# Prompt queries formed by pairs of heads, their rotated part for all heads at once and brought to the heads' rows by DMA

## The reference, cut to what matters

```python
q = (rmsnorm(c_q, ln_q) @ w_q_b).reshape(b, t, N_HEADS_A, QK_NOPE + QK_ROPE)   # 256 -> 8 * (64 + 32)
q_nope = q[..., :QK_NOPE]
q_rope = rope(q[..., QK_NOPE:], pos)      # [x1 * cos - x2 * sin, x1 * sin + x2 * cos]
...
s = einsum(q_lat, ckv) + einsum(q_rope, krope)      # scores; softmax; times the values
```

## Time and profile before

| | |
|---|---|
| median of 3 runs | 798.32 us |
| the profiled execution | 798.34 us, its span 796.5 us |
| PE busy | 767.9 us (96%) |
| PE weight load | 603.7 us (76%) |
| DVE busy | 566.2 us (71%) |
| ACT busy | 411.7 us (52%) |
| POOL busy | 65.0 us (8%) |
| DMA | 65.54 MB, mean 82 GB/s |

### The profile page before, as it was taken

One profiled execution on the slowest core, in us unless ns is written; L12 is line 12 of the kernel. 1 busy time (PEld: TensorE's weight loads), 2 busy tenths in 40 slices (PEclk: granted clock), 3 DMA queues, 4 the chain that ended last, 5 costly groups with the idle time before them and its releaser, 6 DMA issues.

```text
span 796.5 us, 10486 instructions
## 1 busy us (share of the span) xinstructions
PE 767.9 (96%) x3766; PEld 603.7 (76%) x3766; DVE 566.2 (71%) x1093; ACT 411.7 (52%) x942; POOL 65.0 (8%) x114
## 2 busy tenths in 40 slices
PE   6999999999999999999999999999999999999995
PEld 4799877767667578888888988776676756888874
DVE  3348989877877786545463799897878677656477
ACT  3565635654465472353465475457444657323554
POOL 5000123210000220000000011232000000000000
PEclk9999999999999999999999999999999999999998
DMA  8722222100000163422182323211100004341203
GB/s 293 219 72 84 81 69 83 38 27 27 27 1 28 45 206 120 134 80 80 53 259 62 92 88 86 53 57 28 53 14 14 14 14 145 109 144 53 90 17 132
DMA packets 45113, 65.54 MB, mean 82 GB/s; under 512 B 12510, under 2 KB 24634, under 8 KB 45046
## 3 DMA queue, kind: packets, MB, share of 16 engines
q1 hardware_dynamic: 41226, 58.45, 23.3%
q0 software_dynamic: 3776, 6.40, 2.7%
q10 hardware_dynamic: 60, 0.02, 0.0%
HBM read 57.87 MB, written 7.18 MB: 82 GB/s over the span
## 4 chain that ended last, share of the span: by engine, by line
PE 84%; DVE 8%; ACT 5%; issue 2%; DMA 1%; SPq 0%; ACTq 0%; DVEq 0%
PE acc L628 18%; PE acc L630 18%; PE acc L629 18%; PE sharedT L562 4%; PE acc L748 4%; PE sharedT L810 3%; PE sharedS L823 3%; PE sharedO L837 3%; PE sharedS L562 2%; PE sharedO L562 2%; DVE WLO L1379 1%; ACT WHI L1003 1%; DVE VT L1444 1%; PE sharedS L796 1%; PE sharedS L797 1%
## 5 line engine op out<-in xcount | busy, mean ns | idle before, releaser
L628 PE MATMUL acc<-WHI,XHI 128*128 128x512 f32 (+1 forms) x710 | 309.0, 435 | 0.9 <-DVE XLO L1389 0.9
L630 PE MATMUL acc<-WHI,XLO 128*128 128x512 f32 (+1 forms) x710 | 275.3, 388 | 0.0
L629 PE MATMUL acc<-WLO,XHI 128*128 128x512 f32 (+1 forms) x710 | 274.7, 387 | 0.0
L1444 DVE SCALAR_TENSOR_TENSOR VT<-UX,CWT,VT 128x640 f32<-128x640 f32 x240 | 211.8, 883 | 5.4
L628 PEld LDWEIGHTS acc<-WHI,XHI 128*128 128x128 f32 x710 | 133.9, 189 | 33.8 <-issue 8.6
L1379 DVE SCALAR_TENSOR_TENSOR WLO<-WR,GT,WHI 128x512 fp32r<-128x512 f32 (+1 forms) x142 | 98.6, 736 | 82.6 <-ACT WHI L1003 82.2
L629 PEld LDWEIGHTS acc<-WLO,XHI 128*128 128x128 f32 x710 | 134.2, 189 | 30.5 <-issue 8.6
L630 PEld LDWEIGHTS acc<-WHI,XLO 128*128 128x128 f32 x710 | 133.6, 188 | 26.4
L1003 ACT ACTIVATE WHI<-WR,GT 128x512 fp32r<-128x512 f32 (+1 forms) x142 | 93.5, 710 | 95.9 <-PE acc L630 90.9
L1196 ACT ACTIVATE SB<-SB,NBIAS 128x384 f32<-128x384 f32 (+1 forms) x80 | 45.7, 572 | 39.3 <-DVE NBIAS L1500 39.0
L837 PEld LDWEIGHTS sharedO<-V,PT 128*128 128x128 f32 x320 | 44.5, 191 | 16.1 <-issue 8.8
(11 more groups left out here) (207 smaller groups left out, 839.7 us busy)
## 6 DMA issues: line engine op xcount, KB each, us to landing
WR<-in_w_in_dram SPq DMA_DIRECT2D x32, 256.0 KB, 3.0
WR<-in_w_in_dram SPq DMA_DIRECT2D x16, 512.0 KB, 3.7
WR<-in_w_out_dram SPq DMA_DIRECT2D x16, 512.0 KB, 3.6
WR<-in_w_pg_dram SPq DMA_DIRECT2D x16, 512.0 KB, 3.6
WR<-in_w_in_dram SPq DMA_DIRECT2D x8, 416.0 KB, 3.4
residual_spill<-H SPq DMA_DIRECT2D x5, 512.0 KB, 4.1
H<-residual_spill SPq DMA_DIRECT2D x10, 256.0 KB, 3.3
H<-in_x_prompt_dram SPq DMA_DIRECT2D x4, 512.0 KB, 7.6
```

What stands on the lines that cost most here:

```text
L628: mm(out, hi, w_hi, start=(first and k == 0), stop=False)
L629: mm(out, hi, w_lo, start=False, stop=False)
L630: last = mm(out, lo, w_hi, start=False, stop=(final and k == 1))
L1444: ins = stt(out=out, in0=src, scalar=w, in1=out, op0=ALU.mult, op1=ALU.add)
```

## The change

The weights of two heads stand side by side in `WQ` (256 columns a pair: rotated and swapped of the even head, its 64 plain columns, the 64 plain ones of the odd head, rotated and swapped of the odd head). `queries(h)` now forms the plain rows of two heads, for even h alone; their copy has two instructions of 64 rows, on DVE for h = 0, on ACT for h = 2, 4, 6. The rotated part of all heads is two products, `rotated_queries(0)` and `(1)`, with weights that POOL gathers (`WQR`); DVE forms four products with cos and sin, and POOL sends them by DMA through DRAM (`q_spill`) to rows 64 to 127 of `QH`, head by head. `uk0` and `uk1` become one bank use with 4 transposes in place of 8; the cache's rotated keys are flipped by one transpose in place of two; three taps of "g13" move to units 16, 18 and 22. `QH` has three slots.

```diff
@@ tables and bank order
-("z5", ..., "q0", "q1", "g13"), (1, 4, 5, 5, 5, 6, 6, 2, 2, 8)
+("z5", ..., "q0", "q1", "g13"), (1, 4, 5, 5, 5, 6, 6, 2, 2, 5)
-for _u, _m in enumerate((1, 3, 3, 2, 0, 2, 3, 2, 1, 2, 3, 1, 1, 3, 3, 2, 1, 2, 0, 2, 2, 2, 1, 2)):
+for _u, _m in enumerate((1, 3, 3, 2, 0, 2, 3, 2, 1, 2, 3, 1, 1, 3, 3, 2, 2, 2, 1, 2, 2, 2, 2, 2)):
-        cyc(*((l, n) for n in ("taps", "uk0", "uk1", "st0", "st1", "p0", "p1", "p2")))
+        cyc(*((l, n) for n in ("taps", "uk", "st0", "st1", "p0", "p1", "p2")))
+        order["S"].append((l, ("qr", 0)))
+        order["O"].append((l, ("qr", 1)))
-            if i == 2 and h < HEADS - 1:
+            if i == 2 and h in (1, 3, 5):
                 order["T"].append((l, ("q", h + 1)))
@@ loads, SP and POOL
+                src = a["w_q_b"][l, P * k:P * (k + 1), :].rearrange("p (g x e) -> p x g e", g=HEADS // 2, x=2)
+                eng.dma_start(WQ[:, k, :, 128:224], src[:, 1]).then_inc(wq_in, 16)
+                eng.dma_start(WQ[:, k, :, 64:128], src[:, 0, :, 0:NOPE]).then_inc(wq_in, 16)
+                eng.dma_start(WQ[:, k, :, 0:ROPE], src[:, 0, :, NOPE:]).then_inc(wq_in, 16)
@@ TensorE
-                    for j in range(4):
-                        last = flip(quad(name)[0:NOPE, j, :], WKV[:, 0, 4 * g + j, :])
+                for j in range(4):
+                    last = flip(quad("uk")[:, j, :], WKV[:, 0, 2 * j:2 * j + 2, :].rearrange("p h e -> p (h e)"))
                 for j in range(2):
                     flip(quad(name)[:, j, :], CKV[:, slot, j, :])
-                    last = flip(quad(name)[:, 2 + j, :], CKR[:, slot, j, :])
+                fill_inc(flip(quad(name)[:, 2, :], CKR[:, slot, :]), (l, name))
+            def rotated_queries(half):
+                name = ("qr", half)
+                fill_wait(pe, (l, name))
+                pe.wait_ge(wqr_ready, 4 * (l + 1))
+                for k in range(2):
+                    w = WQR[:, k, half].rearrange("p g x e -> p (g x e)")
+                    last = mm(bank((l, name))[:, :], w, CQT[:, k, 0:SEQ], start=(k == 0), stop=(k == 1))
+                fill_inc(last, (l, name))
+                    pe.wait_ge(q_rot_in[h % 3], 16 * (h // 3 + 1 + (3, 3, 2)[h % 3] * l))
                 if t == 2:
                     flip_cache(0)
+                    rotated_queries(0)
+                if t == 3:
+                    rotated_queries(1)
-                if i == 2 and h < HEADS - 1:
+                if i == 2 and h in (1, 3, 5):
                     queries(h + 1)
@@ ScalarE: cache_out in three copies, and in step u after probs(u + 1)
+                copy(CTK[:, 0, 0:PAST], bank((l, name))[:, 0:PAST])
+                for j in range(2):
+                    out = copy(CTK[NOPE:P, 1, P * j:P * (j + 1)], quad(name)[NOPE * j:NOPE * (j + 1), 2, :])
+            def queries_out(h):
+                name = ("q", h)
+                filled_wait(act, (l, name))
+                copy(QH[0:NOPE, h % 3, :], bank((l, name))[0:NOPE, :])
+                drain_inc(copy(QH[0:NOPE, (h + 1) % 3, :], bank((l, name))[NOPE:P, :]), (l, name))
+                if i == 2 and h in (1, 3, 5):
+                    queries_out(h + 1)
@@ VectorE: sample queries in three instructions for each half; after gated_u(1), before taps("g13")
+            dve.wait_ge(rope8_in, 32 * (l + 1))
+            filled_wait(dve, (l, ("qr", 0)))
+            x = bank((l, ("qr", 0)))[:, :]
+            tt(QROT[0], x, COS8, ALU.mult).then_inc(q_rotated, 1)
+            drain_inc(tt(QROT[3], x, SIN8, ALU.mult), (l, ("qr", 0)))
+            filled_wait(dve, (l, ("qr", 1)))
+            x = bank((l, ("qr", 1)))[:, :]
+            tt(QROT[1], x, COS8, ALU.mult).then_inc(q_rotated, 1)
+            drain_inc(stt(out=QROT[2], in0=x, scalar=-1.0, in1=SIN8, op0=ALU.mult, op1=ALU.mult), (l, ("qr", 1)))
             taps("g13")
@@ queries_out(0)
-                drain_inc(tt(QH[:, h % 2, :], bank((l, name))[:, :], ROPET[:, 0:SEQ], ALU.mult), (l, name))
+                for a in range(2):
+                    out = nc.vector.tensor_copy(QH[0:NOPE, h + a, :], bank((l, name))[NOPE * a:NOPE * (a + 1), :])
-                if i == 2 and h < HEADS - 1:
-                    queries_out(h + 1)
@@ GpSimd
+            halves_of_rotated()                      # 4 copies of 128x128 into WQR
             pool.wait_ge(latents_ready, l + 1)
+            for x, row in ((COS8, NOPE), (SIN8, P - 16)):
+                src = a["c_ropet"][row:row + 16, 0:SEQ].unsqueeze(0).to_broadcast([HEADS, 16, SEQ])
+                pool.dma_start(x, src).then_inc(rope8_in, 16)
...
+            for x in range(2):
+                copied_wait(pool, (l, ("qr", x)))
+            pool.wait_ge(q_rotated, 2 * (l + 1))
+            for h in range(HEADS):
+                pool.dma_start(q_spill[h].rearrange("x j n -> j x n"), OTOK[NS * h:NS * (h + 1), 0:4, :]).then_inc(q_spilled, 16)
...
+                if s == CACHED:
+                    pool.wait_ge(q_spilled, 16 * HEADS * (l + 1))
+                    rotated(0)
+            filled_wait(pool, (l, ("s", NB - 1)))
+            rotated(1)
+            rotated(2)
             pool.wait_ge(gated, GATES * l + 2 * TILES)
...
+            for h in range(3, HEADS):
+                filled_wait(pool, (l, ("s", NB + 4 * (h - 3) + 3)))
+                rotated(h)
```

More of the change, by code:

```diff
@@ L86, in _take @@
     return out
-TAP = {place: _take(n) for place, n in zip(("z5", "z6", "z7", "z8", "z9", "l10", "l11", "q0", "q1", "g13"), (1, 4, 5, 5, 5, 6, 6, 2, 2, 8))}
+TAP = {place: _take(n) for place, n in zip(("z5", "z6", "z7", "z8", "z9", "l10", "l11", "q0", "q1", "g13"), (1, 4, 5, 5, 5, 6, 6, 2, 2, 5))}
 for _n in range(NB):
@@ L241, in build @@
         KRB = SB[:, 1, 0:32 * TILES].rearrange("p (t a e) -> p t a e", t=TILES, a=2)
+        COS8, SIN8 = SB[:, 0, :], SB[:, 1, :]
+        QROT = [OTOK[:, x, :] for x in range(4)]
         NBIAS = sb("NBIAS", [P, NB + UNITS])
@@ L307, in build @@
         rope_copied = sem("rope_copied")
+        rope8_in = sem("rope8_in")
+        q_rotated = sem("q_rotated")
+        q_spilled = sem("q_spilled")
+        q_rot_in = [sem(f"q_rot_in{slot}") for slot in range(3)]
         lnf_in = sem("lnf_in")
@@ L588, in turn_small @@
                 pe.wait_ge(wkv_in, 32 * (l + 1))
[L589 to L594 removed]
+                fill_wait(pe, (l, "uk"))
+                for j in range(4):
+                    last = flip(quad("uk")[:, j, :], WKV[:, 0, 2 * j:2 * j + 2, :].rearrange("p h e -> p (h e)"))
+                fill_inc(last, (l, "uk"))
                 pe.wait_ge(state_in, 16 * (l + 1))
@@ L809, in queries @@
                 for k in range(2):
-                    last = mm(bank((l, name))[:, :], WQ[:, k, h, :], CQT[:, k, 0:SEQ], start=(k == 0), stop=(k == 1))
+                    last = mm(bank((l, name))[:, :], WQ[:, k, h // 2, 64:192], CQT[:, k, 0:SEQ],
+                              start=(k == 0), stop=(k == 1))
+                fill_inc(last, (l, name))
[6 more added lines that the diff above has]
+                    last = mm(bank((l, name))[:, :], w, CQT[:, k, 0:SEQ], start=(k == 0), stop=(k == 1))
                 fill_inc(last, (l, name))
@@ L855, in tensor_layer @@
             if l == 0:
[L856 to L857 removed]
+                pe.wait_ge(tables_in, 16 * 3)
+                pe.wait_ge(const_set, 9)
             for t in range(TILES):
@@ L1048, in scalar_layer @@
                     high(first_i + 2)
-            for g in range(2):
-                name = f"uk{g}"
-                filled_wait(act, (l, name))
-                drain_inc(copy(UKT[0:NOPE, 4 * g:4 * g + 4, :], quad(name)[0:NOPE, :, :]), (l, name))
+            filled_wait(act, (l, "uk"))
+            for a in range(2):
+                out = copy(UKT[0:NOPE, :, :].rearrange("p (g a) r -> p a g r", a=2)[:, a],
+                           quad("uk")[NOPE * a:NOPE * (a + 1), :, :])
+            drain_inc(out, (l, "uk"))
             for g in range(2):
@@ L1206, in cache_out @@
                 filled_wait(act, (l, name))
-                drain_inc(copy(CTK[:, :, 0:PAST], bank((l, name))[:, :].rearrange("p (a k) -> p a k", a=2)), (l, name))
+                copy(CTK[:, 0, 0:PAST], bank((l, name))[:, 0:PAST])
+                for j in range(2):
+                    out = copy(CTK[NOPE:P, 1, P * j:P * (j + 1)], quad(name)[NOPE * j:NOPE * (j + 1), 2, :])
+                drain_inc(out, (l, name))
             def sample_out(s):
```

81 lines of the change are left out of this document (44 added, 37 removed).

## The result

The changed kernel takes 813.65 us, median of 4 runs (809.97 to 813.97), against 798.42 us of the kernel before on the same chip (4 runs, 798.23 to 798.59): ratio 1.018, 95% interval 1.0151 to 1.021. It is slower, as forecast, but by 1.8% and not by 1.1%: 813.65 lies 2.2 us above the upper end of the range (811.5). The profiled execution took 813.97 us, its span 812.2 us.

What follows compares the result with a forecast made beforehand. PE was taken as the bound (84% of the chain), with DVE and ACT close behind. From 798.34 us, less 10.5 of PE's work, plus 19.0 of new waits (9.5 a layer): 806.8 us, 1.1% slower, range 801.0 to 811.5.

Steps and rivals of the forecast that it cites:

- PE's own work: Both layers: fewer query products and transposes, two rotated products more, one wait of 1.01 us gone; -10.5 us in all.
- Item 1: Sample scores of stream 1 wait for DVE's taps queued behind the rotated products: +2.6 us a layer.
- Item 2: Head 0's queries: two DVE copies of 64x512 drain bank T in place of one product, +0.6 us a layer.
- Item 3: Unit 2: value_rows(3) waits for DVE's mask, so 1.6 of the 1.71 us saved are lost, each layer.
- Item 4: Unit 10: keys(4) starts 1.25 us earlier in place of the query product's 1.71; loss 0.45 us a layer.
- Item 5: Units 16 to 18: two moved taps land on DVE, keys(6) gains only about 0.9 us; loss 0.8 a layer.
- Item 6: Unit 22: query copies on ACT stand behind filler_out and probs, so flip_probs(22) waits; +2.75 us a layer.
- Item 7: Units 6 and 14: flips wait for ACT's query copies, about 0.4 and 0.6 us, together +1.0 a layer.
- Item 9: Unit 26: its old wait of 0.43 us for DVE is given back; -0.5 us a layer.
- Item 8: Sample rotation on DVE makes low(12) later, +0.2 us a layer (0 to 0.4); three ACT cache copies cost 0.
- The granted clock: Rival: four new waits near 2.8 us each bring an equal stretch at 1.2 GHz, +10.8 us, 817.6 us; chance 0.03.
- PE's work does not decide: Rival it answers: PE's work decides, DVE and ACT catch up, 787.8 us, or about 793 with half the small waits; chance 0.09.

Runs made afterwards that it cites:

- experiment 6: Kernel before with only the merged flip of the key weights (four transposes into one bank use, in place of eight into two): 796.80 us, ratio 0.9972.
- experiments 1 and 3: Changed kernel with g13's five taps ahead of DVE's rotated products: 808.03 us; with eight behind them: 821.60 us; with two ahead, three behind: 809.31 us.
- Experiment 8: Changed kernel with six g13 taps ahead of the rotated products, one between, other taps redealt, and ACT's query copy for heads 6 and 7 ahead of filler_out: 794.99 us.
- experiment 5: Changed kernel with one ACT cache copy in place of three behind each cache flip, leaving out part of the computation: 812.20 us, ratio 1.0156.

## Why the prediction was right or wrong

The execution whose clock column shows 1.00 up to PE's last products (810.42 us) can be compared with the kernel before place by place, by the starts of PE's score products in both traces. It starts its sample loop some 0.7 us later than the other profile of the same kernel (117.88 against 117.17 us). All of this arises in the first 17 us: there the 128x512 products take 0.63 us each until 16.1 us, in the other profile only until 12.5 us, and 0.40 from then on. The working below leaves that out: without dips and without that delay the changed kernel takes about 809.6 us, 2.8 above the forecast, and the dips add the rest. (The first profile gives the same from the other side: 813.97 less its three dips of 1.5, 1.4 and 1.5 us is 809.5.)

- **PE's own work**, -10.5: right as far as it can be tested. A fifth of it, the key weights' flip, gave 2.1 us in experiment 6 where 1.9 were forecast for both layers. In layer 0 the scores of stream 0 start at 117.17 us in place of 114.48, 2.69 later; the two rotated products (+3.42), the later `low(12)` (+0.84, below) and what went ahead of them (0.44, 1.01 and 0.11) give 2.70. So the six query weight loads cost nothing either. In the sample loop the six flips gave 0.44 and not 0.66 us a layer: 0.2 too much.
- **Item 1**, 2.6 us: 2.44, by the distance from stream 0's scores to stream 1's (5.11 in place of 2.67), in both layers. Right, by its mechanism too (experiments 1 and 3).
- **Item 2**, 0.6: 0.70. The row of the two copies in the changed kernel is

```profile
167.59 1.39 DVE L1587 COPY QH<-sharedT 64x512 f32<-64x512 f32 x2 [2.46 <-PE sharedT L828]
```

so each costs its full 0.70, not the distance of 0.60 at which two products of 128 rows follow each other.
- **Item 3**, 1.6: all 1.71 of the saved product were lost. **Item 4**, 0.45: 0.43. **Item 5**, 0.8: 0.68. **Item 6**, 2.75: 2.84. **Item 7**, 1.0: 0.42 + 0.54. **Item 9**, -0.5: -0.63. Right: all of them within 0.15.
- **Item 8** is the step that failed in the sum. Its first half was taken as +0.2 (0 to 0.4). The rows of the sample rotation, in the changed kernel's second profile:

```profile
99.02 0.43 DVE L1538 COPY QH<-sharedS 64x256 f32<-64x256 f32 x1
99.46 0.42 DVE L1539 TENSOR_TENSOR QH<-sharedS,ROPET 64x256 f32<-64x256 f32 x1
99.89 0.42 DVE L1540 TENSOR_TENSOR QH<-sharedS,ROPET 128x256 f32<-128x256 f32 x1
100.23 1.79 DVE L1491 SCALAR_TENSOR_TENSOR VT<-UX,CWT,VT 128x640 f32<-128x640 f32 x2
```

and in the kernel before:

```profile
99.90 0.88 DVE L1488 TENSOR_TENSOR QH<-sharedT,ROPET 128x128 f32<-128x128 f32 x4
100.69 0.87 DVE L1444 SCALAR_TENSOR_TENSOR VT<-UX,CWT,VT 128x640 f32<-128x640 f32 x1
```

One half costs DVE 100.23 - 99.02 = 1.21 us in place of 0.79 (100.69 - 99.90), so both halves cost 0.84 us more; I had put both at some 0.4 and taken half of it. And PE had no slack to speak of before `low(12)` (none in layer 0, 0.2 us in layer 1), so it became waits of 0.85 and 0.63 us: 1.1 us too little for both layers. Experiment 8, with one tap less ahead of `low(12)`, has neither wait. Its second half, "ACT is idle before most of them: 0", failed because one is enough: the cache copies ahead of the last but one `sample_values` stand before a filled stretch of ACT's list, and PE waited 0.65 us more for `PT` in each layer (experiment 5: 1.3 us for both). These two terms are 2.4 of the 2.8 us.

- **The granted clock** is the other failed step: 4.1 us of the 6.9 between 806.8 and 813.65, by difference. A clock below 1.00 outside the ends was among the prediction's own signs of being wrong, and it came. I had it as a rival with a chance of 0.03, because in the first 8 us of the kernel before the column shows 1.00 though PE has 1.38 us of work. That column was misread. The timeline of PE in the kernel before has, for the same product at the start and a little later:

```profile
12.56 0.63 PE L629 MATMUL acc<-WLO,XHI 128*128 128x512 f32 x1
15.30 0.40 PE L629 MATMUL acc<-WLO,XHI 128*128 128x512 f32 x1
```

So after its first 6.6 idle us this PE does run at the lower level, though the column shows 1.00 there: the durations are the witness, and they were in the trace of before. The row of the last 6 us, at 0.67, bore on the case too, and I gave it no weight. The price was wrong as well: not an equal stretch per wait (2.7 us), but 1.2 to 1.5 us, in 13 waits of 22. Where the Trainium skill ("TensorE: Matmul & The Clock Gate", Part 1) has idle time bring the lower level, the trace agrees.
- **The range** took in the items' own bounds, some 3 us either way, but nothing for an effect that can only lengthen. With four waits near 2.8 us, each somewhat over a coin's throw at 1.5 us, the expected surcharge is 3 to 4 us (an estimate from the counts above), and with all four the upper end had to be near 817.
- **The rivals.** PE's work does not decide as the lists stand; experiment 8 shows that 3.9 of its 10.5 us come out once the larger covers are filled. That one of the large waits was missing: no, both stood in both layers. The clock's rival came at about half its price, and so did further small waits. Neither alone leaves the range (806.8 + 4.1 and 806.8 + 2.8 are both under 811.5); it took the two together.

## What to carry to other kernels

When an engine's list gets a wait for a product that is not there yet, look at what stands behind that wait and could stand ahead of it: here five taps and one copy, moved by a few lines, were worth 12 us of a loss of 15. A saving on the bounding engine can come back whole as a wait in the same place, as that of unit 2's query product did, and is then had only together with a new deal of the other engines' work; the merged flip was had at once (experiment 6). And a wait of PE of 2.6 us or more, the shortest here that brought it, has a second price, the lower clock behind it, that varies from one execution to the next: count it at its chance, and make the range wider upwards.

## What the runs showed of the hardware

- A wait of 2.6 to 2.8 us brought the lower level of TensorE's clock in 13 cases of 22, of the same program and the same place now with and now without, for some 3 us and a loss of 1.2 to 1.5 us; waits of 5.4 us brought it in both cases, for over 6 us and a loss of 2.5 us. No wait of 1.75 us or less in mid-kernel brought it. Nine executions of one program took 809.97 and 810.42 us at a mean clock of 0.997 and 0.998, and 811.99 to 815.53 us at 0.989 to 0.993.
- Two DVE instructions follow each other at less than their duration (0.60 for 0.69 us at 128x512; 0.34 for 0.42 at 128x256), but at all of it (0.70, 0.43) where the second starts at other rows than the first. The Trainium skill ("VectorE: DVE Perf Modes", "Two Vector instructions with no wait between them") says that an instruction whose input or output starts in another group of 32 partitions than the last one's is held until that has finished; the trace agrees in the three places shown. I had not applied it, and it makes copies of half the rows cost more than half.
